# A two-block model kernel: the scale row of layer 0 summed in column quarters, with reordered side work

## The reference

```python
# layer 0 of the first block, c is one row of 2048 numbers
mod = silu(c) @ mod_w[0] + mod_b[0]          # 6144 numbers
shift, scale, gate = split(mod, 3)           # 2048 each, in this order in mod_w
h = rms_norm(x, norm_g[0]) * (1 + scale) + shift
v, g = split(h @ pool_w_in, 2)               # 2048 x 4096 weights
mixed = pooled(v) per group @ pool_w_grp * pool_scale
x = x + gate * ((mixed * silu(g)) @ pool_w_out)
# layer 1 begins in the same way, with mod_w[1] and norm_g[1]
```

## Time and profile before

| what | value |
|---|---|
| median of 3 runs | 2357.99 us (2357.73 to 2362.3) |
| profiled execution | 2359.24 us |
| its span on the core | 2357.0 us |
| TensorE busy | 2310.9 us, 98% of the span |
| VectorE busy | 1531.7 us, 65% |
| ScalarE busy | 1134.5 us, 48% |
| moved by DMA | 547 MB, mean 232 GB/s |

### The profile page before, as it was taken

How to read it: one execution, slowest core, us unless ns; L and a number is a source line. 1 busy time by engine, 2 the same in 40 slices (tenths; PEclk the granted TensorE clock), 3 DMA queues, 4 the chain that set the end, 5 groups by cost and what they waited for, 6 DMA issues and landing times.

```text
span 2357.0 us, 29852 instructions
## 1 busy us (share of the span) xinstructions
PE 2310.9 (98%) x10728; PEld 1874.2 (80%) x10728; DVE 1531.7 (65%) x1863; ACT 1134.5 (48%) x1371; POOL 297.5 (13%) x597
## 2 busy tenths in 40 slices
PE   5999999999999999999999999999999999999998
PEld 1877778888788878888888888888888888888886
DVE  2988888666697566775765444665665565565566
ACT  1544444444444456545455444454544444444444
POOL 0000000033300003200031000210231121121120
PEclk8999999999999999999999999999999999999999
DMA  9999996567698547766465766665666666666663
GB/s 391 387 381 373 375 399 253 182 197 222 206 391 274 173 149 235 227 184 183 140 205 169 239 190 194 213 197 188 194 216 204 200 213 197 207 213 195 208 209 112
DMA packets 263659, 547.14 MB, mean 232 GB/s; under 512 B 30188, under 2 KB 30452, under 8 KB 259576
## 3 DMA queue, kind: packets, MB, share of 16 engines
q1 hardware_dynamic: 241520, 510.40, 65.3%
q0 software_dynamic: 20368, 32.58, 4.2%
q10 hardware_dynamic: 1656, 2.66, 0.3%
HBM read 520.36 MB, written 6.30 MB: 223 GB/s over the span
## 4 chain that ended last, share of the span: by engine, by line
PE 89%; DVE 4%; ACT 2%; DMA 2%; issue 1%; POOL 1%; ACTq 0%; DVEq 0%
PE ps L2112 28%; PE ps L2114 28%; PE ps L2113 28%; DMA ifb<-in_f_bias 1%; DVE w_lo L1176 1%; PE ps L2196 1%; PE ps L2230 1%; POOL T L499 1%; PE ps L2409 1%; DMA T<-T 0%; ACT w_hi L568 0%; PE ps L2450 0%; PE ps L2309 0%; PE ps L2386 0%; ACT tmp L898 0%
## 5 line engine op out<-in xcount | busy, mean ns | idle before, releaser
L1176 DVE TENSOR_TENSOR w_lo<-raw,w_hi 128x1024 fp32r<-128x1024 f32 x784 | 945.5, 1216 | 564.2 <-ACT w_hi L568 549.9
L568 ACT CAST w_hi<-raw 128x1024 fp32r<-128x1024 f32 x784 | 814.9, 1046 | 849.6 <-PE ps L2114 801.2
L2112 PE MATMUL ps<-w_hi,xa_hi 128*128 128x512 f32 x2176 | 854.3, 393 | 6.1 <-DVE w_lo L1176 5.0
L2114 PE MATMUL ps<-w_hi,xa_lo 128*128 128x512 f32 x2176 | 847.3, 389 | 0.0
L2113 PE MATMUL ps<-w_lo,xa_hi 128*128 128x512 f32 x2176 | 846.9, 389 | 0.0
L2112 PEld LDWEIGHTS ps<-w_hi,xa_hi 128*128 128x128 f32 x2176 | 408.5, 188 | 100.8 <-issue 9.7
L2114 PEld LDWEIGHTS ps<-w_hi,xa_lo 128*128 128x128 f32 x2176 | 408.4, 188 | 85.6
L2113 PEld LDWEIGHTS ps<-w_lo,xa_hi 128*128 128x128 f32 x2176 | 408.6, 188 | 83.1
L499 POOL DMA_DIRECT2D T<-T x576 | 282.2, 498 | 1182.7 <-DVE T L1276 1029.1
L2112 PE MATMUL ps<-w_hi,xb_hi 128*128 128x512 f32 x928 | 364.2, 392 | 0.9 <-DVE w_lo L1176 0.5
L2114 PE MATMUL ps<-w_hi,xb_lo 128*128 128x512 f32 x928 | 361.3, 389 | 0.0
(11 more groups left out here) (273 smaller groups left out, 1004.1 us busy)
## 6 DMA issues: line engine op xcount, KB each, us to landing
raw<-in_w_in SPq DMA_DIRECT2D x176, 512.0 KB, 4.0
T<-in_mod_w SPq DMA_DIRECT2D x160, 512.0 KB, 7.8
raw<-in_attn_w_in SPq DMA_DIRECT2D x144, 512.0 KB, 4.6
raw<-in_w_up SPq DMA_DIRECT2D x128, 512.0 KB, 4.3
raw<-in_w_down SPq DMA_DIRECT2D x128, 512.0 KB, 4.7
raw<-in_pool_w_in SPq DMA_DIRECT2D x64, 512.0 KB, 8.5
T<-T POOLq DMA_DIRECT2D x576, 32.0 KB, 3.8
T<-in_mod_w SPq DMA_DIRECT2D x16, 1024.0 KB, 9.1
```

The source lines that it names most:

```text
L568: nc.scalar.copy(w_hi[:, o % SPL, :, 0:cols], raw[:, o % RAW, :, 0:cols]).then_inc(hi_ready, 1)
L1176: tt(w_lo[:, o % SPL, :, part], raw[:, o % RAW, :, part], w_hi[:, o % SPL, :, part].bitcast(F32), ALU.subtract).then_inc(lo_ready, 1)
L2112: mm(dst, x_hi, h, start=first and k == 0, stop=False)
L2114: ins = mm(dst, x_lo, h, start=False, stop=last and k == KPC - 1)
```

## The change

**Scale row in quarters.** The 16 pieces of 1 MB become 32 pieces of 0.52 MB (`M0`): two input rows of a partition by 512 columns. Eight pieces make one quarter of the columns. There are six slots; piece m waits until m - 5 pieces are taken. x comes ahead of them on SyncE's queue, in two tiles. Behind pieces 6 and 7 of a quarter comes one weight chunk of block 0 each. TensorE runs quarter 0, then chunks 0 and 1, then quarter 1, chunks 2 and 3, and so on (`quarter_piece`, `quarter_columns`); a piece is 8 matmuls of 128 columns. VectorE makes a quarter's scale and then the low part of its group (`quarter_scale`).

**Around it.** ScalarE issues its 17 small loads ahead of silu(c). The rotary work comes behind quarter 0. Riders begin at chunk 8 and not at chunk 4. All 32 PE pieces lie in pool_gate and pool_out (8 lay in the group stage). The shift of layer 0 starts two to three chunks later. At the seam the shift row of layer 1 is summed by `total_rows`, copied to `mod_rows2` and turned to columns by `mod_columns`. The last block of mix_out runs its chunks 4 to 7 tile by tile, and the first tile's square and weighting run beside the second tile.

```diff
-    at = [v + c for c in range(4, 32) for _ in range(2 if c in (11, 17, 23, 28) else 1)]
+    at = [v + c for c in range(8, 36) for _ in range(2 if c in (11, 17, 23, 28) else 1)]
...
-    return at, [first["group"] + i for i in range(8)] + [gate + 1 + i * 60 // 24 for i in range(24)]
+    return at, [gate + 1 + i * 60 // 32 for i in range(32)]
...
-            for k in range(KC):
-                if k >= 4:
-                    sp.wait_ge(mod_taken, k - 3)
-                sp.dma_start(mod_raw[:, k % 4, :], mws[0][:, 1, k, :]).then_inc(mod_landed[k % 4], 16)
+            for t, arrived in enumerate((x_landed, x_second)):
+                sp.dma_start(T0[:, t, :], x[0, t * P:(t + 1) * P, :]).then_inc(arrived, 16)
+            for m in range(M0):
+                if m >= 6:
+                    sp.wait_ge(mod_taken, m - 5)
+                i, col = m % 8, m // 8 * NBLK
+                sp.dma_start(mod_raw[m % 6].rearrange("p (k n) -> p k n", k=2), mws[0][:, 1, 2 * i:2 * i + 2, col:col + NBLK]
+                             ).then_inc(mod_landed[m % 6], 16)
+                if i >= 6:
+                    load(SOURCES["pool_v"], 0, m // 8 * 2 + i - 6, 0, first=True)
...
+            def quarter_scale(q):
+                bank, part = 3 - q % 2, slice(4 * q, 4 * q + 4)
+                dve.wait_ge(mod_taken, 8 * q + 8)
+                nc.vector.tensor_copy(q_raw[:, q * P:q * P + P], ps[:, bank, 0:P]).then_inc(q_rows, 1)
+                dve.wait_ge(q_sum, q + 1)
+                step(tt(scl[:, 0, part], ps[:, bank, S:S + 4], MODB[0][:, part], ALU.add))
+                step(tt(scl[:, 0, part], scl[:, 0, part], G0[:, part], ALU.mult))
+                dve.sem_inc(q_scl, 1)
+                norm0_low(q)
...
-                4: shift_rows, 5: shift0_start, 6: lambda: shift0_next(0),
-                7: lambda: shift0_next(1), 8: lambda: shift0_next(2), 9: lambda: shift0_next(3)})
+                4: lambda: low_job(SPLITS["pool_v"] + 3, XB, 3, 4), 7: shift_rows, 8: shift0_start,
+                9: lambda: shift0_next(0), 10: lambda: shift0_next(1)})
+            shift0_next(2)
+            shift0_next(3)
...
+            def quarter_piece(q, i):
+                m = 8 * q + i
+                pe.wait_ge(mod_landed[m % 6], 16 * (m // 6 + 1))
+                for k in range(2):
+                    col = csil[:, 2 * i + k:2 * i + k + 1].to_broadcast([P, 32])
+                    for r in range(4):
+                        at = k * NBLK + r * P
+                        ins = mm(ps[32 * r:32 * r + 32, 3 - q % 2, 0:P], col, mod_raw[m % 6][:, at:at + P],
+                                 start=i == 0 and k == 0, stop=i == 7 and k == 1, skip_group_check=True)
+                ins.then_inc(mod_taken, 1)
...
+                if i == 5:
                     pe.wait_ge(vec_done, 1)
-                    hooks.pop(-1)()
+                    norm_job("norm0", 0, xn, 0)
...
-            phase("pool_v", XA, pool, first=hooks, ready=SPLITS["norm0"], half=1)
+            for j in range(CPB):
+                if j == 0:
+                    pe.wait_ge(x_first, 1)
+                else:
+                    pe.wait_ge(x_ready, SPLITS["norm0"] + j // 2 + 1)
+                chunk(0, j, XA, KPC * j, 0, j == 0, j == CPB - 1)
+                if j in (0, 2):
+                    norm_job("norm0", 0, xn, 2 + j // 2)
+                if j in (1, 3, 5):
+                    q = (j + 1) // 2
+                    if q >= 2:
+                        pe.wait_ge(q_scl, q - 1)
+                    for i in range(8):
+                        quarter_piece(q, i)
+                    quarter_columns(q)
...
-            total(3, 6, 0)
-            mod_columns(3, 7, KC, True)
+            total_rows(3, 6)
+            mod_columns(2, 7, KC, True)
             awake(4)
+            mod_columns(3, 6, 0, False, mod_rows2)
+            pe.wait_ge(root_ready, 2)
+            awake(3)
...
+            def by_tiles(B, A, X, tile):
+                pe.wait_ge(acc_free, A - 1)
+                for j in range(4):
+                    chunk(B, j, X, KPC * j, A, j == 0, False)
+                for t in range(NT):
+                    for j in range(4, CPB):
+                        chunk(B, j, X, KPC * j, A, False, j == CPB - 1, (t,),
+                              w_used if t else tile if j == CPB - 1 else None)
```

More of the change, by code:

```diff
@@ L37 @@
 N_FFN = 8
+M0 = 32
 C_ID, C_TRI, C_CUM, C_ONE, C_FRQ = 0, 128, 512, 640, 768
@@ L84, in _pe_slots @@
     late = sum(chunk < edge for chunk in PE_CHUNK)
-    slots = [4, 6, 5, 7] + [q % 4 for q in range(4, late)]
+    slots = [q % 4 for q in range(late)]
     slots += [(2, 3, 4, 5, 6, 7)[i % 6] for i in range(32 - late)]
@@ L99, in _pe_issue @@
     for q in range(32):
[L100 to L103, removed]
+        if PE_PREV[q] is None:
+            g = group + RAW + (4 if PE_SLOT[q] < 2 else 7)
+            if PE_SLOT[q] >= 4:
+                g = PHASES["pool_out"][0] * CPB + RAW + 1
         else:
             g = PE_CHUNK[PE_PREV[q]] + RAW + 3
-            if PE_SLOT[q] >= 4 and PE_PREV[q] < 4:
-                g = PHASES["pool_out"][0] * CPB + RAW + 1
         at.append(max(g, at[-1]) if at else g)
@@ L783, in _ @@
                     mixed((o - 5) // 2)
-                if o >= 6 and o < 10:
-                    shift0(o - 6)
+                if o >= 9:
+                    shift0(o - 9)
             mixed(3)
+            shift0(2)
+            shift0(3)
             XA, XB = SECOND, FIRST
@@ L1093, in _, with mix_tile_square @@
                 mix_out(b, b + B0, b + A0)
-            blk(B0 + n - 1)
+            def mix_tile_square():
+                act.wait_ge(mix_tile, 1)
+                act.wait_ge(mix_part, 1)
+                square(SQ["mix_out"] + 3 * NT, ps[:, (A0 + n - 1) % 2 * 2, :], ms_part[:, 0, 0, n - 1:n], junk_a)
+            blk(B0 + n - 1, {8: mix_tile_square})
             act.wait_ge(w_used, (B0 + n) * CPB)
-            for t in range(NT):
-                if t:
-                    act.wait_ge(mix_part, 1)
-                square(SQ["mix_out"] + 3 * NT + t, ps[:, (A0 + n - 1) % 2 * 2 + t, :], ms_part[:, 0, t, n - 1:n], junk_a)
+            square(SQ["mix_out"] + 3 * NT + 1, ps[:, (A0 + n - 1) % 2 * 2 + 1, :], ms_part[:, 0, 1, n - 1:n], junk_a)
             root(5, NT)
@@ L1445, in _, with scale_rows @@
             dve.wait_ge(csil_ready, 1)
-            def scale_rows(i, bank, taken, of=mod_taken):
+            def scale_rows(i, bank, taken, of=mod_taken, to=mod_rows):
                 dve.wait_ge(of, taken)
-                nc.vector.tensor_copy(mod_rows, ps[:, bank, :]).then_inc(rows_ready, 1)
+                nc.vector.tensor_copy(to, ps[:, bank, :]).then_inc(rows_ready, 1)
             def scale(i, sums, src, g):
@@ L2014, in sums_next @@
             def sums_next():
-                sums(*next(rest))
+                t, a, z = next(rest)
+                if t and z == D:
+                    mix_last(1)
+                    dve.sem_inc(res_done, 1)
+                    dve.sem_inc(acc_free, 1)
+                sums(t, a, z)
             def ffn_rstd():
@@ L2257, in total_rows @@
                 ins.then_inc(sum_rows, 1)
-            def total(u, bank, col):
-                pe.wait_ge(mod_used, RIDE[u] + 2 * KC)
-                for f in range(KC):
-                    ins = mm(ps[:, bank, col + f:col + f + 1], mod_acc[u][:, f * P:(f + 1) * P], ones[:, 0:1],
-                             start=True, stop=True)
-                ins.then_inc(mod_sum, 1)
             def total_gate(u, rows, banks):
@@ L2279, in awake, with quarter_columns @@
                     mm(ps[:, 1, 0:P], ident, ident, start=True, stop=True)
-            hooks = feed("norm0", 0, xn)
+            def quarter_piece(q, i):
[8 more added lines that the diff above has]
+                ins.then_inc(mod_taken, 1)
+            def quarter_columns(q):
+                pe.wait_ge(q_rows, q + 1)
+                mm(ps[:, 3 - q % 2, S:S + 4], q_raw[:, q * P:q * P + P], ident[:, 0:P:32], start=True, stop=True
+                   ).then_inc(q_sum, 1)
             pe.wait_ge(csil_ready, 1)
-            for k in range(KC):
-                mod_piece(k, mod_raw[:, k % 4, :], 3, 0, NBLK, mod_landed[k % 4], 16 * (k // 4 + 1), k == 0)
-                if k == 7:
+            for i in range(8):
+                quarter_piece(0, i)
+                if i == 3:
                     pe.wait_ge(vec_landed, 16 * 13)
@@ L2564, in _ @@
                 branch(b)
-            phase("mix_out", XB, first={3: lambda: job(JOBS["branch"], stage, staged, STAGED["branch"] + 4, bank=4)}, ready=SPLITS["branch"])
+            B0, A0, n = PHASES["mix_out"]
+            blk(B0, A0, XB, True, {3: lambda: job(JOBS["branch"], stage, staged, STAGED["branch"] + 4, bank=4)}, SPLITS["branch"])
+            with pe.Fori(1, n - 1) as b:
+                blk(b + B0, b + A0, XB, True)
+            by_tiles(B0 + n - 1, A0 + n - 1, XB, mix_tile)
             X0 = SPLITS["ffn"]
```

124 lines of the change are left out of this document (63 added, 61 removed).

## The result

The changed kernel takes 2384.64 us (median of 5 runs, 2382.39 to 2386.56), the kernel before 2357.73 on the same chip (2356.81 to 2362.3). The ratio is 1.0113, with an interval of 1.0102 to 1.0125: slower by 26.9 us. The profiled execution took 2382.39 us.

The account below looks back on a forecast made before the run. It took TensorE to bound the kernel from the first chunk to pool_out's end, with everything earlier paid in full. Terms 16.6 + 2.5 + 1.5 - 2.6 - 0.4 = +17.6 us gave a median of 2375.6 us, range 2358 to 2388.

Parts of the forecast that it names:

- the pieces of a turn: Layer 0's start: after the chunks, a quarter's pieces, with landing of the last ones, cost TensorE 7.9 us per turn.
- Chunk 0: Start of the kernel: first chunk begins at 31.6 us (bounds 29 and 33), 28 us sooner than before.
- The turn: Layer 0's start: each further quarter costs 20.4 us for pieces, scale, two chunks and clock, three times.
- From sum to chunk: Within a turn: copy, product, scale and the writes before the next chunk take 4.9 us (bounds 4.5 and 5.9).
- Two chunks with their job: Within a turn: two chunks 5.6 us, a transposing job 0.7, and 2.0 for the clock.
- Chunk 8: Start of the second block: at 99.8 us against 83.23, a term of +16.6 us.
- The clock: TensorE's low clock in the turns at the start: a loss of 2.0 us per pair of chunks (0 to 2.8).
- The shift: Layer 0's shift starts later, so TensorE waits for VectorE's splits queued behind it: +2.5 us (0 to 3.5).
- Riders and pieces: Eight more units in pool_gate and pool_out, where DMA engines are full; late riders hold VectorE's splits: +1.5 us (0 to 5).
- The seam before idx_q: Summing by `total_rows` instead of `total` leaves TensorE less work ahead of idx_q: -2.6 us (-1 to -3.2).
- The end of mix_out: Last block by tiles, one tile's square and weighting done early: -0.4 us (-0.9 to 0).
- The faster rival: Start of layer 0: quarters come at the DMA's pace, chunk 8 near 72.5 us, time 2348 us; chance 0.10.

Follow-up runs that it names:

- slots8: The changed kernel with eight slots for pieces instead of six, and the first rider row cleared later: 2366.91 us, ratio 1.0044.
- pieces: The changed kernel with TensorE's first eight pieces back in the group stage, as before the change: 2380.55 us, ratio 1.0096.
- ahead8p: The changed kernel with TensorE taking pieces one quarter ahead, eight slots, and the first eight pieces back in the group stage: 2358.31 us, ratio 1.0002.
- seams: The kernel before with only the change's two seams (sum by rows ahead of idx_q, last block of mix_out by tiles): 2356.57 us, ratio 0.999.
- ahead8: The changed kernel with TensorE taking quarter q + 1's pieces ahead of quarter q's chunks, and eight slots: 2362.79 us, ratio 1.0026.

## Why the prediction was right, and where it was off

It said slower, 2375.6 us within 2358 to 2388; the time was 2384.64, 26.9 us more than before and not 17.6. The mechanism held; the sum was too small, most of all in the pieces of a turn.

- **Chunk 0** at 31.6: it was 31.2. Quarter 0 was summed at 28.1 (28.3), and the last steps took 3.1 for 3.3. That the sum came at the forecast moment is luck: `vec_done` was 1.4 us late, at 23.9 for 22.5, and what followed took 4.2 us for 5.8.
- **The turn** was 20.4: it was 21.7 and 21.2 (chunks 2, 4, 6 at 52.1, 73.8, 95.0). The term that was mis-sized is the pieces, 7.9: they took 9.5, 8.4 and 9.4 us, 3.6 more in the three turns, and that is about the miss at chunk 8. In the first and third turn the eighth piece landed 3.7 and 3.6 us behind the seventh, for 2 x 1.37, and in the second 2.7. In the first the weight chunk's issue took 1.73 us; its load waits for nothing in the program, and the cause stays open. From sum to chunk was 4.8 for 4.9, three times. Two chunks with their job took 8.5 us, for 8.3 (5.6, 0.7 and 2.0 for the clock). Chunk 8: +19.9 for +16.6.
- **The clock** was 2.0 a pair, 6.0 in all. It was 0.50 in each turn (46 to 56 us, for one; 10.2, 10.2 and 13.7 us long), and keeping it up moved chunk 8 by 6.4. What I missed is that this is worth less in the end, since the transfers behind are the next bound. The rule that I weighed, of the Trainium skill, "TensorE: Matmul & The Clock Gate", section "HAM oscillation — how this bites in real kernels", holds in this trace: each turn of short bursts with a wait for DMA fell back to the low clock. It fell in each turn of `slots8` too, where TensorE waited for no piece, for 3.4, 6.8 and 6.8 us. The lower bound of the term, 0, came from a misread row: the trace of the kernel before has no record of the clock ahead of 26.4 us, and the view prints 1.00 there. The products tell that it was low in that stretch: in the kernel before, the same eight instructions took

```profile
14.42 1.93 PE L2230 MATMUL ps<-T,csil 128*32 128x512 f32 x8 [3.32 <-DMA T<-in_mod_w]
...
27.79 1.06 PE L2230 MATMUL ps<-T,csil 128*32 128x512 f32 x8 [1.11 <-DMA T<-in_mod_w]
```

- **The shift**, +2.5: from chunk 8 to 40 the shift is -3.9 us, of which the eight pieces taken out of the group stage are -6.3 (a piece costs TensorE 0.79 us: chunks of 3.38 and 2.85 where others take 2.72), so +2.5. Behind chunk 40 comes a wait of 0.82 us for chunk 43's `w_lo`, which the prediction had in this term too. That makes 3.3 for 2.5, within its bounds of 0 to 3.5.

```profile
212.40 0.50 PE L2137 MATMUL ps<-w_hi,xa_hi 128*128 128x512 f32 x1 [0.82 <-DVE w_lo L1186]
```

- **Riders and pieces**, +1.5: from chunk 40 to 103 it is +10.4; the eight pieces moved there are 6.3, chunk 43's wait is 0.8, and 3.3 are left, of which waits for `w_lo` at chunks 91, 95 and 99 are 2.3. The term was mis-sized by 1.8, within its bounds of 0 to 5; `pieces` and `ahead8p` took back 2.2 and 2.5 us. I had also priced a piece at 0.64, its own duration, and not by how far it pushes the next chunk.
- **The seam before idx_q**, -2.6: it is -2.6, for another cause. The step that failed is "4.87 - 1.1 us less on TensorE, of which 2 to 3 come through": nothing of it comes through at equal clock. That the number agrees is luck.
- **The end of mix_out**, -0.4: from the start of mix_out's last product to that of the next chunk's first it was 7.15 us and is 6.33, but 0.9 is given back 14 us later, in a wait for `w_lo` of 0.68 us, in `seams` as in the changed kernel, so the term is 0. VectorE's second weighting has moved between the splits there.

```profile
1682.89 0.47 PE L2137 MATMUL ps<-w_hi,xb_hi 128*128 128x512 f32 x1 [0.68 <-DVE w_lo L1186]
```

The moments add to +23.6 in the profile. The other 3.3 us to the medians' 26.9 are spread of single executions: before, the profiled one lay 1.5 us above its median, after it 2.3 below. The faster rival (2348, chunk 8 at 72.5) was not reached in any run: with the DMA engines hardly idle chunk 8 is at 81.7, or 78.9 with the clock kept up and a debt behind it. I had counted the 44 units from 0 us at full rate; in `ahead8` the last piece landed at 67.6 us, not at 61.

What stays open: the later places of shift and riders cost 3.8 us in `ahead8p`, and no run takes them away or parts the two; and whether other moments could give the old sum a seam over 15.6 us.

## What to carry to other kernels

Before you start an engine sooner, ask what fills the time ahead of it. Here the DMA engines were busy from the first microseconds to the end of the stage: an earlier first product saved next to nothing, and the gaps that the interleaving left in the transfers were lost nearly one for one in four kernels. Buffer a whole turn (eight slots, not six), so that the transfers already issued last until the consumer is back. Side work belongs where transfers idle: eight pieces moved out of such a stage cost 2.2 and 2.5 us in the traces. And price a short instruction by how far it moves the next long one.

## What the runs showed of the hardware that I had not expected

- At the seam before idx_q the low spell of TensorE's clock came in lengths of 3.4, 6.8 and 10.2 us, and the same code drew 10.2, 10.2 and 6.8 us in the kernel before, 3.4 and 6.8 with the new places, by the moment it ran. Thirty-two products of one column took 4.87 us in the first case and 3.63 with the clock high.
- From 10 to 20 us the rate fell to 323 GB/s at a DMA share of 0.96 after the change, for 414 at 1.02 before. In that stretch 989 packets are under 512 B, for 226 before, and all are under 8 KB, for 398 of 893 before; no run parts the two.
- An issue on SyncE's queue that waits for one slot kept weight chunks that wait for nothing themselves behind it for 9.9 and 13.6 us.
